# A hybrid encoder block on one core: the scaled residual joins the output projection's sums, and the first norm reads PSUM

## What is computed

```python
proj = jnp.einsum('bsd,de->bse', x, w_in)
y_ml = _mlstm_group(...)        # 4 heads, both directions
y_ssm = _mamba2_group(...)      # 16 heads, both directions
mix = jnp.einsum('bse,ed->bsd', jnp.concatenate([y_ml, y_ssm], axis=-1), w_out)
h = _layer_norm(ALPHA * x + mix, ln1_g, ln1_b)      # ALPHA = 2 ** 0.25
ffn = _moe(h, ...)              # 64 experts, 8 per token, one shared expert
return _layer_norm(ALPHA * h + ffn, ln2_g, ln2_b)
```

## Time and profile before

| what | value |
|---|---|
| runs | 819.32, 819.67, 816.76 us; median 819.32 us |
| profiled execution | 819.9 us, its span 817.8 us |
| mean granted TensorE clock over the span | 0.964 of full speed |
| TensorE matmul busy | 738.7 us, 90% of the span |
| VectorE busy | 266.9 us, 33% |
| ScalarE busy | 157.3 us, 19% |
| DMA, mean over the span | 307 GB/s, 251.45 MB moved |

### The profile page before, as it was taken

How to read it: one execution, slowest core, us unless ns; L and a number is a source line. 1 busy time by engine, 2 the same in 40 slices (tenths; PEclk the granted TensorE clock), 3 DMA queues, 4 the chain that set the end, 5 groups by cost and what they waited for, 6 DMA issues and landing times.

```text
span 817.8 us, 11133 instructions
## 1 busy us (share of the span) xinstructions
PE 738.7 (90%) x4548; PEld 436.4 (53%) x4548; DVE 266.9 (33%) x676; ACT 157.3 (19%) x335; POOL 37.4 (5%) x50
## 2 busy tenths in 40 slices
PE   4999999599999999899999997996996996999971
PEld 3888888478994445454444453443443443444520
DVE  2501696446653057321221221111111121222216
ACT  0010431404642013221111121111111111111201
POOL 1020000520200011000000000000000000000000
PEclk9999999799999999999999999898899998999987
DMA  8953444443421387999999999999999999999921
GB/s 293 386 193 146 155 155 144 138 182 106 151 78 40 154 349 282 394 389 386 371 412 426 422 428 424 427 424 423 428 425 423 426 425 426 424 422 428 424 121 51
DMA packets 27330, 251.45 MB, mean 307 GB/s; under 512 B 3601, under 2 KB 3873, under 8 KB 6033
## 3 DMA queue, kind: packets, MB, share of 16 engines
q1 hardware_dynamic: 24704, 240.78, 72.0%
q0 software_dynamic: 2576, 9.98, 3.6%
HBM read 249.76 MB, written 1.11 MB: 307 GB/s over the span
## 4 chain that ended last, share of the span: by engine, by line
PE 71%; DMA 22%; DVE 4%; ACT 1%; issue 1%; SPq 1%; POOL 0%; DVEq 0%
PE bank L593 20%; DMA arena<-in_we_dram 19%; PE bank L896 19%; PE bank L938 7%; PE bank L717 6%; PE bank L849 5%; PE bank L858 4%; PE bank L692 3%; DMA arena<-in_wc_dram 2%; PE bank L766 1%; PE bank L671 1%; PE bank L914 1%; PE bank L807 1%; DMA arena<-decay_rows 1%; ACT bank L994 1%
## 5 line engine op out<-in xcount | busy, mean ns | idle before, releaser
L896 PE MATMUL bank<-arena 128*64 128x512 f32 (+1 forms) x1024 | 194.4, 647 | 33.6 <-DMA arena<-in_we_dram 33.6
L593 PE MATMUL bank<-arena 128*128 128x256 f32 x768 | 169.3, 382 | 2.7 <-DMA arena<-in_wc_dram 2.7
L593 PEld LDWEIGHTS bank<-arena 128*128 128x128 f32 x768 | 146.8, 192 | 23.3 <-DMA arena<-in_wc_dram 3.1
L896 PEld LDWEIGHTS bank<-arena 128*64 128x64 f32 (+1 forms) x1024 | 54.1, 132 | 132.2 <-issue 129.7
L938 PE MATMUL bank<-arena 128*64 128x512 f32 (+1 forms) x512 | 91.3, 597 | 0.7 <-issue 0.7
L849 PEld LDWEIGHTS bank<-onehotb,h_part 128*128 128x128 bf16 x1248 | 69.8, 98 | 20.3 <-issue 20.3
L1483 DVE COPY arena<-bank 64x1 f32<-64x1 f32 (+1 forms) x64 | 9.9, 155 | 211.0 <-PE bank L914 210.3
L849 PE MATMUL bank<-onehotb,h_part 128*128 128x128 bf16 x1248 | 74.2, 219 | 0.8 <-ACT arena L1095 0.8
L1502 DVE TENSOR_TENSOR y_lo<-bank,y_hi 128x512 fp32r<-128x512 f32 x50 | 34.6, 692 | 100.9 <-ACT y_hi L1122 75.2
L717 PE MATMUL bank<-arena 128*128 128x512 f32 x128 | 55.7, 593 | 0.3 <-DVE arena L1195 0.3
L938 PEld LDWEIGHTS bank<-arena 128*64 128x64 f32 (+1 forms) x512 | 25.8, 125 | 52.8 <-issue 46.3
(11 more groups left out here) (235 smaller groups left out, 497.2 us busy)
## 6 DMA issues: line engine op xcount, KB each, us to landing
arena<-in_we_dram SPq DMA_DIRECT2D x64, 2048.0 KB, 20.7
arena<-in_we_dram SPq DMA_DIRECT2D x64, 1024.0 KB, 26.3
arena<-in_wc_dram SPq DMA_DIRECT2D x12, 1024.0 KB, 15.8
arena<-in_wn_dram SPq DMA_DIRECT2D x12, 1024.0 KB, 4.7
arena<-in_wo_dram SPq DMA_DIRECT2D x8, 1024.0 KB, 4.7
arena<-decay_rows POOLq DMA_DIRECT2D x5, 1024.0 KB, 6.8
arena<-in_ln_dram POOLq DMA_DIRECT2D x2, 1024.0 KB, 8.5
arena<-in_ws_dram SPq DMA_DIRECT2D x1, 2048.0 KB, 8.6
```

Source lines behind the costliest of these rows:

```text
L593: mm = nc.tensor.matmul(bank[n % 2][:, j * S:(j + 1) * S], wk, xk, start=(k == 0), stop=(k == KD - 1))
L896: mm = nc.tensor.matmul(bank[0][rows[q], :], hc[v][:, k, rows[q]], slot[places[q]][:, k * 512:(k + 1) * 512], start=(k == 0), stop=(k == K ...
```

## The change

Four things:

- A second identity, `ident_a`, is the first one times ALPHA. VectorE makes it once, behind the copy of line 1238 and ahead of the score copies, and signals `scaled_ident`.
- TensorE waits for x and for `ident_a` after k = 11. Ahead of k = 12 to 15 of each tile it multiplies `ident_a` with the two halves of x's tile and accumulates into the same banks (`start=False`). The banks then hold ALPHA * x + mix.
- VectorE's first norm is written out. bn_stats reads each bank, and the centring is two operations of 512 columns from the banks into h. The scale-and-add of line 1356 is gone from this norm; its wait for x is gone too.
- The second norm still uses `layer_norm`, unchanged.

```diff
--- before.py
+++ after.py
@@ -232,6 +232,7 @@
         eid = nc.alloc_sbuf_tensor_at("eid", [P, NJ], I32, offset=arena_at + 4 * (O_ROWS + 592))
 
         ident = small("ident", [P, P])
+        ident_a = small("ident_a", [P, P])
         identb = small("identb", [P, P], BF16)
         negm = small("negm", [P, 2, P], BF16)
         zb = small("zb", [P, P], BF16)
@@ -270,6 +271,7 @@
         s_gatew = [sem(f"s_gatew{i}") for i in range(2)]
         s_late = sem("s_late")
         s_xin = sem("s_xin")
+        scaled_ident = sem("scaled_ident")
         s_out = sem("s_out")
         s_shared = sem("s_shared")
         s_shdown = sem("s_shdown")
@@ -734,7 +736,13 @@
                 if k in (KD + 1, KD + 3):
 
                     y_transpose(k // 2 + 2)
+
+            pe.wait_ge(s_xin, 16)
+            pe.wait_ge(scaled_ident, 1)
             for t in range(T):
+                for half in range(2):
+                    nc.tensor.matmul(bank[2 * t + half][:, :], ident_a[:], xin[:, t, half * 512:(half + 1) * 512],
+                                     start=False, stop=False)
                 for k in range(12, 2 * KD):
                     mm = project(k, t)
                 mm.then_inc(mix_used, 1)
@@ -1236,6 +1244,8 @@
             cols = bank[5][:, 0:4 * R].rearrange("p (i d r) -> p i d r", i=2 * T, d=2)
             terms = colT.rearrange("p (i d) r -> p i d r", d=2)
             V.tensor_copy(terms, cols[:, :, :, 0:SH + H]).then_inc(misc_evac, 1)
+            dve.wait_ge(s_ident, 16)
+            V.tensor_scalar(ident_a[:], ident[:], ALPHA, None, ALU.mult).then_inc(scaled_ident, 1)
             dve.wait_ge(s_conv, 32)
             for hd in range(H):
                 misc_copy(M_ST + hd, st[:, hd, :, :], mbank(M_ST + hd, 2))
@@ -1368,9 +1378,22 @@
                                            op0=ALU.mult, op1=ALU.add).then_inc(signal, 1)
                 dve.wait_ge(signal, T)
 
-            dve.wait_ge(s_xin, 16)
             dve.wait_ge(s_late, 16)
-            layer_norm(xin, h, ln1, 3, h_ready, 0, mix_used, (OUNITS - 1, OUNITS))
+            for t in range(T):
+                dve.wait_ge(mix_used, OUNITS - 1 + t)
+                for half in range(2):
+                    link(V.bn_stats(stat[:, 2 * t + half, :], bank[2 * t + half][:, :]))
+                link(V.bn_aggr(mv[:, t, :], stat[:, 2 * t:2 * t + 2, :].rearrange("p a b -> p (a b)")))
+                V.tensor_scalar(vv[:, 0, t:t + 1], mv[:, t, 1:2], EPS, None, ALU.add).then_inc(var_ready, 1)
+                dve.wait_ge(var_ready, 3 + t)
+                for half in range(2):
+                    c = slice(half * 512, (half + 1) * 512)
+                    link(V.scalar_tensor_tensor(out=h[:, t, c], in0=bank[2 * t + half][:, :], scalar=mv[:, t, 0:1],
+                                                in1=ln1[:, 0, c], op0=ALU.subtract, op1=ALU.mult))
+                rsqrt(slice(t, t + 1), 3 + t)
+                V.scalar_tensor_tensor(out=h[:, t, :], in0=h[:, t, :], scalar=vv[:, 3, t:t + 1], in1=ln1[:, 1, :],
+                                       op0=ALU.mult, op1=ALU.add).then_inc(h_ready, 1)
+            dve.wait_ge(h_ready, T)
             def top_k(t):
 
                 dve.wait_ge(score_ready, t + 1)
```

## The result

The changed kernel takes 820.44 us (median of 10 runs, 818.73 to 824.87); the kernel before, in 10 runs, the three known before the forecast among them, 816.81 us (816.07 to 819.67). The medians differ by 3.6 us. The ratio is 1.0049, 95% interval 1.0029 to 1.0068, that is 4.0 us, between 2.4 and 5.6: slower, clear of noise. The forecast was 819.3 + 2.6 = 821.9 us, range 819.2 to 824.4. The time lies in the range, the ratio at the edge of what I had called no change. Part of the agreement in absolute time is luck: with more runs the median of before moved from 819.32 down to 816.81 us, so the shift to compare is 2.6 forecast against 3.6 measured.

The account below looks back on a forecast made before the run. The end is set by the expert-weight stream, which TensorE starts, so early TensorE delays reach the end. 3.47 − 0.23 − 0.3 − 0.3 = +2.6 us on 819.3 gives 821.9 us, range 819.2 to 824.4.

Parts of the forecast that it names:

- Step 1 and 2: Making ident_a on VectorE, at most 0.49 us, and TensorE's new waits for x and ident_a: nothing at the end.
- Step 3: TensorE's four float32 products, two ahead of each tile, cost 3.47 us in all, with nothing hiding them.
- Step 4: VectorE's first norm per tile: 5.7 us against 6.9, with 512-wide centring from PSUM at 0.75 us and bn_stats 0.69.
- Step 5: From the norms to the routers, TensorE ends last, not VectorE; after small give-backs everything stands at +2.6 us.
- h copy terms: ScalarE's bf16 copy runs before the transposes, so its h copies follow sooner: −0.3 us for each of two tiles.
- wait at router(0): TensorE's idle time at 302.32 us, before tile 0's h transposes, would be absorbed: −0.23 us.
- slack of tile 1's norm: Tile 1's norm on VectorE would end at 311.4 us, 0.65 us before TensorE reaches router(1).
- rival D: ScalarE's relief does not come or is larger: +3.2 or +2.2 us; counted within the forecast's 0.64 chance.
- A (half price): TensorE's products leave one record each, four costing 1.74 us: +0.9 us, 820.2 us; chance 0.08.
- B (VectorE last): Tile 1's VectorE chain exceeds 6.4 us, at 7.9, and delays router(1) by 4.5 us: 823.8 us; chance 0.10.
- C (the stream moves by experts 2 and 3 alone): DMA queue never empty after 302 us, so those loads' +3.5 us sets the end: 822.8 us; chance 0.10.
- E (the cost drowns): Run scatter hides the whole kernel's added cost; the median could stand at 819.3 us; chance 0.08.

Follow-up runs that it names:

- longer chain: The change with two more unused statistics operations on VectorE in each tile's first norm; median 824.15 us, ratio 1.0076 to the kernel before.
- products twice: The change with ident_a at half the scale and every product made twice, eight in all; median 822.97 us, ratio 1.0058 to the kernel before.
- ident_a alone: The kernel before, with ident_a allocated and made by VectorE but used by nobody; median 817.27 us, ratio 0.9996.
- profile 3 of the change: The unedited change, profiled once more; one run of 821.97 us, stage 31.73 us, 501.59 us behind the stage.
- tile 1 alone: The change made for tile 1 only, two products, tile 0's norm as before; median 818.98 us, ratio 1.0008 to the kernel before.
- zero products: The kernel before plus the four TensorE products with an identity times 0, VectorE's norm unchanged; median 823.94 us, ratio 1.0069.
- h copies first: The kernel before, with ScalarE's h copies ahead of its bf16 copy of the same tile; median 820.31 us, ratio 1.0027.

## Why the prediction came out as it did

**What bounds the kernel: right.** Doubling the products moved the stage by 3.44 us and nothing came back in the 500 us behind it (500.04 against 499.96 us).

**Step 1 and 2, ident_a and the new waits, at nothing: right** (ratio 0.9996; no wait at 285.72 us).

**Step 3, products: right**, 3.43 us for 3.47.

**Step 4, VectorE's prices: right**, 0.751 and 0.700 us. The Trainium skill's fixed costs of 120 cycles for a PSUM source and 58 for SBUF ("VectorE: DVE Perf Modes", section on the SBUF-source errata) would, by my estimate, have made bn_stats 65 ns dearer than its 0.694 us from SBUF; it is 6 ns dearer. The 131 ns per pass of the Trainium skill's "TensorE: Matmul & The Clock Gate" (section on the back-to-back issue gap) is as far off as before: a record here is 0.429 us, 214 ns a pass if it holds two.

**Step 5, who is last: right in kind, the sum 0.4 us too high.** The forecast was 3.47 − 0.23 − 0.3 − 0.3 = 2.6 us. Measured: 3.43 − 0.39 − 0.29 − 0.28 − 0.27 = 2.20 us. Both h copy terms are as forecast. The wait at router(0) before was worth 0.39 us, not the 0.23 that the idle time in the row shows: from the start of the last group to the next instruction, 32 records at 0.429 us make 13.74 us, and 14.13 had passed. And one give-back was missed: router(1) too had waited 0.28 us for VectorE before (line 759 to router(1) took 4.75 us, now 4.47), although its row shows no idle time. The chain of waits quoted at the head of the prediction said so: it ran through VectorE from 302.27 to 309.09 us, right up to router(1). Yet the sum took 309.13 as a time that TensorE set. The ends of matmul groups in the rows reach over the next start (285.72 + 1.88 = 287.60, and the next group starts at 287.44), so short waits vanish from the idle column; the spacing of starts keeps them. Because TensorE thus reaches router(1) earlier than the sum says, the slack of tile 1's norm is 0.27 us and not the 0.65 that was forecast. The 2.2 us that rival D names is the stage's number, but D gives it to a larger relief on ScalarE, which did not come.

**Rivals.** A (half price) fell, with eight records of full length. B (VectorE last) fell by 0.27 us of slack, its mechanism shown by the longer chain. C (the stream moves by experts 2 and 3 alone) would give the 3.5 us that the medians show, and still fell: the hole stayed, and with C the stretch behind the stage would have to be some 1.2 us longer with four products, with two and with eight alike, but it is 499.96, 499.10 and 500.04 us against 500.09. E (the cost drowns) fell: the intervals start at 1.0029 and 1.0031.

**The size of the whole: 0.7 to 1.0 us too small by the medians.** Two measurements give 3.6 and 3.3 us (4.0 and 3.9 by their ratios), with intervals of 2.4 to 5.6 and 2.5 to 5.2 us; the stage gives 2.20 or 2.21 in every profile. So 1.1 to 1.8 us lie outside the stage, if they are real: 2.4 us, the lower end, would leave next to nothing. At the same mean clock over the span the change is 2.7 us above before (0.966: 820.0 us in 7 runs, 817.3 in 14), 3.0 us (0.964: 820.7 in 4, 817.7 in 24) and 3.7 us (0.962: 822.7 in 6, 819.0 in 18), all runs with a clock on record taken together. At the highest clock half a microsecond is left over, and it grows where the clock was lower. Nor do the medians of the other versions follow their stages: against before they are 1.0 us under the stage's difference with the products twice, and 2.1 us over it with the longer chain.

I did not find the place of the rest: not ident_a, not the clock in the router stretch of the profiled executions. What the sum lacks is a term for everything outside the stage, which the prediction puts at nothing (it names such a shift among its signs of being wrong). Whether and where it is stays open. There are too few profiles of the kernel before, one and the one with ident_a alone, to set against five of the change: starts of 288.19 and 286.15 against 285.72 to 286.66 us, rests of 500.09 and 499.33 against 499.96 to 501.59 us. The rest is 0.8 us longer on average with the change, but that average rests on two profiles: ident_a alone with its short last wait for weights, and profile 3 of the change with its lost clock. The kernel before, with 500.09 us, lies among those of the change, and the longer chain, which has all four products, has the shortest rest, 499.05 us. So the profiles show no place where the change alone is slower outside the stage.

None of the versions beats the kernel before. The nearest that moves work is the change for tile 1 alone, 0.5 us longer in the stage.

## What to carry to other kernels

Before moving work to the matrix engine, ask whether it stops anywhere in that stretch. Here the products cost their full 3.43 us, and the 1.2 us per tile that they spared VectorE could pay back only the 0.39 and 0.28 us for which TensorE had waited on it. Add up waits by the spacing of starts, not by the idle column. And a run of VectorE between two engines may depend on a third: look at what GpSimd does at the same moment before reordering anything.

## What had not been expected of the hardware

- VectorE's 1024-wide operation with both inputs in SBUF took 2.89 instead of 1.28 us while GpSimd subtracted two SBUF tensors (303.27 to 305.40 us).
- TensorE's granted clock fell to the 1.2 GHz level for 6.8 us behind a stretch in which it was busy 2.84 of 4 us and its longest waits were 0.76 and 0.97 us (zero products), and again for 6.8 us behind a wait of 1.90 us (h copies first); with 1.05 and 0.97 us (longer chain) it did not, in the one profile taken.
- Behind TensorE's last wait for expert weights, 40 records of equal work took 7.24 us after a wait of 5.41 us and 6.20 us after one of 4.38 us, with a clock of 0.50 and 0.61 over the first 4 us.
- A float32r product of 512 columns costs 0.24 us, the average of eight, a float32 one 0.86 us, so that two float32r parts of a value cost TensorE 0.48 us.
